# The last group's four tiles go through merge, output, query and routing one by one

## The reference

```python
mix = g[:, :, 0] * (o_sb @ w_br_sb) + g[:, :, 1] * (o_nsa @ w_br_nsa) + g[:, :, 2] * (o_moba @ w_br_moba)
x = layer_norm(DEEPNORM_ALPHA * x + mix @ w_out, ln1_g, ln1_b)
return layer_norm(DEEPNORM_ALPHA * x + peer_ffn(x, peer_wq, peer_k1, peer_k2, peer_u, peer_v), ln2_g, ln2_b)

# peer_ffn, per block of 128 tokens
q = jnp.einsum('td,dhc->thc', xb, w_q)
s1 = jnp.einsum('thc,hkc->thk', q[..., :half], sub_k1).astype(jnp.float32)
s2 = jnp.einsum('thc,hkc->thk', q[..., half:], sub_k2).astype(jnp.float32)
...                                    # top 8 of each, top 8 of their 64 sums: 4 heads x 8 = 32 experts a token
act = jax.nn.gelu(jnp.einsum('thkd,td->thk', u_tab[idx], xb).astype(jnp.float32))
return jnp.einsum('thk,thkd->td', (g * act).astype(v_tab.dtype), v_tab[idx])
```

## Time and profile before

| what | us |
|---|---|
| median of 3 runs | 2807.62 |
| profiled execution, span (first to last instruction) | 2819.9 |
| its own time | the page gives the span alone; the slowest of the three runs is 2830.58 |
| end of the last tile's attention (copy of its output, L1431) | 2456.9 |
| last index stored (L1643) | 2571.8 |
| TensorE, VectorE, ScalarE, GpSimd busy | 2453.4, 1942.6, 786.9, 1233.1 |
| transfers | 777 MB, mean 276 GB/s |

### The profile page before, as it was taken

The page is one execution under the profiler, slowest core; times in us unless marked ns, Lnnn a source line. Parts: engine busy times, 40 slices in busy tenths (PEclk is TensorE's granted clock), DMA queues, the critical chain, the costliest instruction groups (busy, mean ns, idle before and its releaser), DMA issues.

```text
span 2819.9 us, 30185 instructions
## 1 busy us (share of the span) xinstructions
PE 2453.4 (87%) x10632; PEld 1484.2 (53%) x10632; DVE 1942.6 (69%) x4009; ACT 786.9 (28%) x1563; POOL 1233.1 (44%) x1028
## 2 busy tenths in 40 slices
PE   8998998998999989899988887999989999987126
PEld 4764476575445357657654465476445347644012
DVE  0122245588988875667886887587998886687875
ACT  2243222213344332321342212212445333301001
POOL 0000023354565432434553655164656352656775
PEclk9998999999989999999997998999999899999569
DMA  4323258787888776977896999787889685998998
GB/s 144 105 73 100 90 188 337 273 290 253 304 283 302 266 251 224 379 286 270 323 359 246 338 375 350 272 297 255 298 297 330 221 308 200 394 366 317 362 373 320
DMA packets 224183, 776.98 MB, mean 276 GB/s; under 512 B 23200, under 2 KB 39712, under 8 KB 219552
## 3 DMA queue, kind: packets, MB, share of 16 engines
q0 software_dynamic: 147456, 536.94, 52.1%
q1 hardware_dynamic: 73696, 227.80, 22.6%
q10 hardware_dynamic: 2880, 10.31, 0.9%
HBM read 766.56 MB, written 8.39 MB: 275 GB/s over the span
## 4 chain that ended last, share of the span: by engine, by line
PE 57%; DVE 15%; DMA 9%; issue 8%; POOL 7%; ACT 3%; another core or an unknown queue 0%; DVEq 0%; ACTq 0%; SPq 0%
PE ps L1056 14%; PE ps L931 7%; PE ps L900 6%; PE ps L984 6%; PE ps L1089 5%; POOL rows L840 4%; DVE x L1535 4%; DMA rows<-in_table_u,idx 4%; PE ps L886 3%; DMA rows<-in_table_v,idx 3%; PE ps L1124 3%; DVE rows L1520 2%; PE ps L1150 2%; DMA wring<-in_merge 2%; PE ps L993 2%
## 5 line engine op out<-in xcount | busy, mean ns | idle before, releaser
L840 POOL DMA_INDIRECT rows<-in_table_u,idx x462 | 565.2, 1223 | 1021.3 <-DVE idx L1643 506.7
L1056 PE MATMUL ps<-xT,wring 128*128 128x256 f32 x3072 | 768.1, 399 | 56.5 <-DMA wring<-in_merge 24.6
L840 POOL DMA_INDIRECT rows<-in_table_v,idx x434 | 526.5, 1213 | 490.5 <-DVE x L1535 362.4
L1056 PEld LDWEIGHTS ps<-xT,wring 128*128 128x128 f32 x3072 | 586.2, 197 | 245.4 <-issue 90.4
L1520 DVE CUSTOM_DVE_ANT_0 rows<-rows,x 128x1024 f32<-128x1024 f32 x462 | 555.0, 1223 | 120.0 <-DMA rows<-in_table_u,idx 114.3
L1535 DVE SCALAR_TENSOR_TENSOR x<-rows,wts,x 128x1024 f32<-128x1024 f32 x413 | 529.8, 1283 | 65.6 <-DMA rows<-in_table_v,idx 43.6
L1089 PE MATMUL ps<-KA,QA 33*128 33x512 f32 (+7 forms) x576 | 253.7, 537 | 26.5 <-DVE part_m L1777 12.9
L1389 ACT ACTIVATE scratch<-scratch,negm 128x640 f32<-128x640 f32 (+7 forms) x192 | 143.5, 747 | 475.3 <-DVE negm L1777 464.6
L900 PE MATMUL ps<-wring,G 128*128 128x512 f32 x384 | 184.8, 617 | 9.7 <-DVE G L1678 6.3
L1777 DVE CUSTOM_DVE_ANT_0 scratch<-ps,cst 128x128 f32<-128x128 f32 (+3 forms) x192 | 86.9, 454 | 143.0 <-PE ps L1089 140.3
L886 PE MATMUL ps<-oT,wring 128*128 128x256 f32 x384 | 126.0, 464 | 53.0 <-DVE G L1673 35.1
(11 more groups left out here) (209 smaller groups left out, 2951.4 us busy)
## 6 DMA issues: line engine op xcount, KB each, us to landing
wring<-in_merge SPq DMA_DIRECT2D x216, 512.0 KB
wring<-in_w_out_h SPq DMA_DIRECT2D x48, 512.0 KB
wring<-in_w_query SPq DMA_DIRECT2D x32, 512.0 KB
G<-in_w_query SPq DMA_DIRECT2D x12, 1024.0 KB, 8.5
G<-in_x SPq DMA_DIRECT2D x16, 512.0 KB, 4.6
G<-in_ln SPq DMA_DIRECT2D x8, 1024.0 KB, 6.8
G<-x_mid SPq DMA_DIRECT2D x16, 512.0 KB, 5.4
rows<-in_table_u,idx POOLq DMA_INDIRECT x462
```

Of the source, the lines that this page charges most:

```text
L840: pool.indirect_dma_start(row_slot(n), None, tab_u if table == "u" else tab_v, bass.IndirectOffsetOnAxis(ap=idx[:, GT * (g % 2) + t, e:e + ...
L1056: mm = pe.matmul(gate_bank(p)[:, SW * n:SW * (n + 1)], w[:, lo:lo + P], xT[:, kc, SW * (p // HALF_GATES):SW * (p // HALF_GATES + 1)], star ...
```

## The change

The last group has four sections of one tile instead of two of a pair. Tile 12's runs in phase 2, tile 13's in phase 3, tile 14's in phase 4, and tile 15's after the last attention. The gates stay in halves of 256 tokens: the first 12 gate steps go into phases 0 and 1 (six each), steps 12 to 15 into phase 3 behind tile 13's section, 16 to 23 into phase 4 ahead of tile 14's. The tanh stays one for a half. In groups 0 to 2 the whole first section moves into phase 3, the score statistics there take its first half, and the gates 12 to 23 are all in phase 4. Merge follows the tanh at once everywhere. `route` takes its work buffers from a free part of `G` and no longer waits for attention. The last group loads every section's weights through the ring (20 pieces each). The planner's constants change, expert rows of the last group go tile by tile (u, v, u, v), and a tile's gelu follows at the first step of its v block.

```diff
+LAST_GROUP = [(0,), (1,), (2,), (3,)]
+SECTIONS = [(g, tiles) for g in range(NG - 1) for tiles in ((0, 1), (2, 3))] + [(NG - 1, tiles) for tiles in LAST_GROUP]
...
+def home_half(sec):
+    return {"first": 1, "third": 0}.get(role(sec), gate_half(sec))
...
 def early_section():
-    first = [("tanh", 0, 0, 0.0)] + [("gate", 0, (HALF_GATES, part), 0.0) for part in range(PARTS)]
-    first += gate_steps(HALF_GATES + 1) + [("merge", 0, k, 1.5) for k in range(12)] + section_outs(0) + gate_steps(HALF_GATES + 2)
-    second = [("norm", 0, 1, 0.0)] + gate_steps(HALF_GATES + 3)
-    second += [("turn", 0, k, 1.5) for k in range(2 * ST)] + sum([query_steps(0, k) for k in range(4)], [])
-    second += [("match", 0, k, 1.2) for k in range(2 * ST)] + [("route", 0, tt, 0.5) for tt in range(ST)]
-    return first, second + sum([gate_steps(p) for p in range(HALF_GATES + 4, GATES)], [])
+    first = [("tanh", 0, 0, 0.0)] + [("merge", 0, k, 1.5) for k in range(12)] + section_outs(0)
+    first += [("norm", 0, 1, 0.0)] + [("turn", 0, k, 1.5) for k in range(2 * ST)] + sum([query_steps(0, k) for k in range(4)], [])
+    return first + [("match", 0, k, 1.2) for k in range(2 * ST)] + [("route", 0, tt, 0.5) for tt in range(ST)]
...
+def tile_section(s, begin=False):
+    steps = [("tanh", s, 0, 0.0)] if begin else []
+    steps += [("merge", s, k, 1.5) for k in range(6)] + section_outs(s, 1) + [("norm", s, 0, 0.0)]
+    steps += [("turn", s, k, 1.5) for k in range(2)] + sum([query_steps(s, k) for k in range(2)], [])
+    return steps + [("match", s, k, 1.2) for k in range(2)] + [("route", s, 0, 0.5)]
...
-    share = [0, 5, 9, 12]
+    share = [0, 5, 9, 12] if g + 1 < NG else [0, 6, 12, 12]
...
+        elif g + 1 < NG:
+            late = sum([gate_steps(p) for p in range(HALF_GATES, GATES)], [])
+            streams.append((0.0, early_section() if phase == 3 else late, 0.97))
+        elif phase == 2:
+            streams.append((0.0, tile_section(0, True), 0.97))
+        elif phase == 3:
+            streams.append((0.0, tile_section(1) + sum([gate_steps(p) for p in range(HALF_GATES, HALF_GATES + 4)], []), 0.97))
         else:
-            streams.append((0.0, early_section()[phase - 3], 0.95))
+            own = tile_section(2, True) if len(LAST_GROUP) == 4 else []
+            streams.append((0.0, sum([gate_steps(p) for p in range(HALF_GATES + 4, GATES)], []) + own, 0.97))
...
-            streams.append((0.0, row_steps(phase, GT * half + phase), 0.85))
+            streams.append((0.0, row_steps(phase, GT * half + phase), 0.5 if phase == 3 and g + 1 < NG else 0.85))
...
+BLOCKS = [(sec, table, t) for sec, (g, tiles) in enumerate(SECTIONS) for table in ("u", "v") for t in tiles]
...
-            if kind == "tanh" and sec >= NS:
-                nxt = max(nxt, SECTION_STEPS * (sec - NS + 1) + 19)
+            if kind == "tanh" or kind == "merge" and a == 0:
+                nxt = max(nxt, steps_needed(sec))
...
-            now += (.78 if kind in HEAD_KINDS or s < 0 else 1.12 if not late else 1.0 if g % 2 else 1.1) * pe
+            now += (.78 if kind in HEAD_KINDS or s < 0 else 1.12 if not late else 1.05) * pe
             if kind in ("tanh", "turn") and s < 0:
-                ahead = 1.0 if g == NG else TIGHT_AHEAD if kind == "tanh" else EXPERT_AHEAD
+                ahead = TIGHT_AHEAD if kind == "tanh" else EXPERT_AHEAD
+            if g >= NG - 1 and s >= 0 and kind in ("merge", "turn") and role(sec) in ("third", "last"):
+                ahead = 0.5 if kind == "merge" or g == NG else EXPERT_AHEAD
...
-            if kind == "route" and a == ST - 1:
-                ready, started = SECTION_STEPS * (sec + 1), busy + 8.0
-                if s == 0:
+            if kind == "route" and a == len(SECTIONS[sec][1]) - 1:
+                ready, started = 2 * NEXP * tiles_before(sec + 1), busy + 8.0
+                if sec == NS * g and g < NG:
                     times.append(started)
-                    if g == NG - 1:
-                        ahead = 1.0
...
         def piece(sec, kind, k):
-            if SECTIONS[sec][1] > 0:
+            if role(sec) in ("late", "last"):
                 return bank(6 + k % 2)
-            return bank(6 if kind in ("merge", "out") else k % 2)
+            if role(sec) == "third":
+                return bank(k % 2)
+            return bank(6 if role(sec) in ("first", "second") or kind in ("merge", "out") else k % 2)
         def depth(sec, kind):
-            return 1 if SECTIONS[sec][1] == 0 and kind in ("merge", "out") else 2
+            return 1 if role(sec) in ("first", "second") or role(sec) == "early" and kind in ("merge", "out") else 2
...
             def residual(sec):
+                if home_half(sec) != gate_half(sec):
+                    sp.wait_ge(idx_ready, GT * g + tiles[0])
+                else:
+                    sp.wait_ge(x1T_free, sec + 1)
...
+            def ring_section(sec):
+                for b in (2, 1, 0):
+                    load("br", sec, b)
+                if home_half(sec) == gate_half(sec):
+                    residual(sec)
+                for n in range(4):
+                    load("o", sec, n)
+                if home_half(sec) == gate_half(sec):
+                    norm_rows(sec)
+                for n in range(4, 8):
+                    load("o", sec, n)
+                for n in range(8):
+                    load("q", sec, n)
                 load("k", sec)
...
                 for n in GATES_FIRST:
+                    if n == GATES - 4 and role(early[0]) == "first":
+                        residual(early[0])
+                        norm_rows(early[0])
                     load("gate", g, n)
...
                     if n == 2 * GATES - 8:
-                        used(("q", sec, 7))
-                        used(("k", sec))
+                        sp.wait_ge(idx_ready, GT * g + ST)
...
+                        elif role(late[0]) == "third":
+                            residual(late[0])
+                            norm_rows(late[0])
...
-            sp.wait_ge(oT_copied, GT * NG)
-            late_section(NS * NG - 1)
+            for sec in sections_of(NG - 1, 1):
+                ring_section(sec)
...
-                if e == 10 and b > 0:
+                if b > 0 and e == (0 if own_next(b - 1) else 10):
                     expert_finish(b - 1)
...
-            def route(T):
+            def route(sec, T):
-                dve.wait_ge(values_done, pairs_before(GT * g + GT - 1) + 1)
+                home_ = home_half(sec)
+                eqbuf = G[:, 1, home_, 0:512]
+                cand = G[:, 1, home_, 512:768].rearrange("p (h n) -> p h n", h=PH)
```

More of the change, by code:

```diff
@@ L42, with role, sections_of, tiles_before @@
 NS = GT // ST
-SECTIONS = [(g, s) for g in range(NG) for s in range(NS)]
 SW = ST * P
+LAST_GROUP = [(0,), (1,), (2,), (3,)]
+SECTIONS = [(g, tiles) for g in range(NG - 1) for tiles in ((0, 1), (2, 3))] + [(NG - 1, tiles) for tiles in LAST_GROUP]
+LAST = len(SECTIONS) - 1
+def role(sec):
+    g, tiles = SECTIONS[sec]
+    if len(tiles) == 1:
+        return ("first", "second", "third", "last")[tiles[0]]
+    return "early" if tiles[0] == 0 else "late" if g + 1 < NG else "last"
+def sections_of(g, half):
+    return [sec for sec, (own, tiles) in enumerate(SECTIONS) if own == g and tiles[0] // ST == half]
+def tiles_before(sec):
+    return sum(len(tiles) for _, tiles in SECTIONS[:sec])
+def gate_half(sec):
+    return SECTIONS[sec][1][0] // ST
+def home_half(sec):
+    return {"first": 1, "third": 0}.get(role(sec), gate_half(sec))
+def merges_of(sec):
+    return 6 * len(SECTIONS[sec][1])
+def merges_before(sec):
+    return 6 * tiles_before(sec)
+def queries_before(sec):
+    return 2 * tiles_before(sec)
 ITEM = KC * 256
@@ L171, in gate_steps, with section_outs @@
     return [("gate", 0, (p, part), 1.72) for part in range(PARTS)]
-def section_outs(s):
-    out = [[("out", s, (k, part), 1.72) for part in range(PARTS)] for k in range(2 * ST)]
+def section_outs(s, tiles=ST):
+    out = [[("out", s, (k, part), 1.72) for part in range(PARTS)] for k in range(2 * tiles)]
+    if tiles == 1:
+        return out[0] + out[1] + [("mean", s, 0, 0.0)]
     return out[0] + out[1] + out[2] + [("mean", s, 0, 0.0)] + out[3][0:2] + [("norm", s, 0, 0.0)] + out[3][2:4] + [("mean", s, 1, 0.0)]
@@ L215, in head_steps @@
     route = [("route", -1, tt, 0.5) for tt in range(ST)]
-    steps = [("tanh", -1, 0, 0.0)]
     if g == NG:
-        steps += merge + outs + turn[0:2] + norm + turn[2:4]
-        return steps + sum(query, []) + match + route
-    steps += turns[0:2]
+        return pair_section(LAST - NS * NG) if len(SECTIONS[LAST][1]) > 1 else tile_section(LAST - NS * NG)
+    steps = [("tanh", -1, 0, 0.0)] + turns[0:2]
     for n in range(6):
@@ L342, in cost, with steps_needed @@
             "turn": (1.5, 0.0), "query": (1.72, 0.0), "match": (1.2, 0.0), "route": (0.0, 9.0)}[step]
+def steps_needed(sec):
+    g, tiles = SECTIONS[sec]
+    if g == 0:
```

(3 more changed lines are left out.)

332 lines of the change are left out of this document (182 added, 150 removed).

## The result

The changed kernel takes 2921.69 us (median of 4 runs, 2905.25 to 2932.53) against 2806.9 before. The ratio is **1.040**, interval 1.034 to 1.045. Forecast was 2753 us. The profiled execution took 2925.97 us, span 2924.2. The two traces differ by 104 us where the medians differ by 115, since the execution traced before (span 2819.9) lies further above its median.

The account below looks back on a forecast made before the run. TensorE bounds up to 2457 us, DMA after 2572. Attention ends at 2457 + 48 + 24 = 2529, last section 73, 112 rows x 1.417 = 159, + 4: span 2765, 55 below 2819.9; median 2753, range 2713 to 2830.

Parts of the forecast that it names:

- Groups 0 to 2, booked at +19 rows and no time: Groups 0 to 2 route some 45 us earlier, so the plan stands +19 rows (0 to 25) ahead by the last group.
- (b): Last group's stage: merge right behind tanh without gates makes TensorE wait at two places, +6 us (0 to 15).
- Single tiles in the stage: +48: Last group's attention stage: tile 14's section plus splitting tiles 12 and 13, 44 us at the stage's 93%, +48 us.
- New waits in the stage: +24: TensorE in the last group's stage: busier VectorE +8, merge behind tanh +6, later weights +10 us.
- Rows beside attention: Last group's stage: rows filling holes make VectorE busier, costing TensorE +8 us (0 to 12).
- +19 +10 +32 rows: Last group's stage: +19 rows from the filled hole, +10 from the earlier last routing, +32 from attention lasting 72 us longer.
- Weights later: +10 (0 to 40): Attention stage: weights come later as transfers are denser, TensorE waits +10 us (0 to 40) beyond today's 6.5.
- Last section: 73: Tile 15's section after attention, from merge to routing, takes 73 us, with indices at 2602.
- Rest: 112 rows at 1.417: After the last routing 112 expert rows are left at 1.417 us each, 159 us, + 4.
- Rival 2: Transfers bound the attention stage through ring pieces beside gathers; median 2843 (+1.3%), slower by over 1% below 312 GB/s; chance 0.17.
- Rival 3: Short gaps from one-bank pieces lower TensorE's clock from 0.92 to 0.85 over 2067 to 2529; median 2768; chance 0.12.
- The profiled execution: Profile page before the change: its span of 2819.9 was taken for the run of 2830.6, with 10.7 us around it.

Follow-up runs that it names:

- covering run: Changed kernel with other positions in the written order only: attention steps between tanh and merge and between norm and turn, queries' spread ahead of tanh; 2883.82 us, ratio 1.029.
- e_pairs_cover_late: Changed kernel with pairs in the last group, tanh and norm covered by attention steps, last pair's weights loaded as before the change; 2838.98 us, ratio 1.002, slower chip.
- thinned: VectorE works on 128 of 1024 columns of stage rows: old groups 0 to 2 with single-tile last group 2890.16 us (1.017); kernel before 2833.53 us (0.997).
- e_last_small: Old groups 0 to 2, single-tile last group; its stage rows worked on 128 of 1024 columns and gathered at 128 KB instead of 512 KB; 2793.31 us, ratio 0.994.
- lighter run: Old groups 0 to 2, single-tile last group, a quarter of each output and query weight piece of its four sections loaded; 2869.81 us, ratio 1.024.
- repacked pairs: Changed kernel with the last group in two pairs again, laid out like its groups 0 to 2: 2879.87 us, ratio 1.027; with tanh and norm covered: 2839.74 us, 1.009.
- e_lastonly2: Changed kernel's single-tile last group behind groups 0 to 2 laid out as before the change, run as yardstick on another chip; 2885.88 us, ratio 1.028.

## Why the prediction was wrong, step by step

The span was to fall by 55 us and grew by 104, a miss of 159: 57 of it up to the stage, 54 in the stage, 17 in the last section, 31 in the rest. Two steps failed. The repacking of groups 0 to 2 was given no cost, and rows beside attention were given almost none. The other bullets are terms of the sum that were mis-sized, and what was right.

- **Groups 0 to 2, booked at +19 rows and no time**, are the first failed step. I priced only the gain of routing "some 45 us earlier". The first routing came 25 us earlier in group 0, 2 in group 1 and 7 later in group 2. By the plan 21 rows more are indeed done at the end of the last head (599, not 578), but this cost 67 us in this trace, 50 and 54 in the other two of the same groups. The covering run shows 22 to 39 of them as uncovered tanh, norm and the slower clock behind. I had booked (b) at two places of 3 us in the last group; in groups 0 to 2, where the diff takes the same gates away, I booked nothing. And I looked at VectorE's merge, not at ScalarE's queue, where the spread waits behind the tanh. What stays after covering is 28 us by these two traces, and on the slower chip nothing clear (e_pairs_cover_late ends the groups at 1768, the old layout at 1758 to 1771); that inherited rows are its cause is argued, not shown.
- **Single tiles in the stage: +48.** With the rows' work and transfers nearly taken away the stage is 606 us, 47 above the 559 of before with its full rows, so this is a floor for the excess. With 225 rows (before: 230) it is 631, +72. By matmuls the step was nearly right: TensorE is busy 55 us more in that run, where 44 were reckoned. One slip: by columns alone the sum would be 7 us smaller, not 5 (88 matmuls for each of three tiles, 0.027 us each).
- **New waits in the stage: +24.** TensorE is idle 53 us more. The norm's end makes 24 of them, a wait that the sum had only in the last section. The merge product makes 18 (booked: 6) and the spread behind the tanh 7. Covering alone did not shorten the stage, so these waits are where the time shows and not shown to be its cause.
- **Rows beside attention, booked as almost free,** are the second failed step. I counted +19 +10 +32 rows in the stage at 8 us of price, and the other rows as taking idle VectorE time. The last 51 rows (276 against 225) cost the stage 60 us, 1.2 us each; in the tail a row costs 1.4 to 1.5. A row moved forward gains 0.3 to 0.6, not 1.417. The thinned and the small-row runs show that the larger part of the price is in transfers: VectorE's own time is 14 to 33 us, the transfers 52 to 63.
- **Weights later: +10 (0 to 40)** was booked as TensorE waiting for weights. That wait did not grow: 4.4 + 1.1 us in the stage instead of 6.5. The lighter run allows up to 10 us for the weights' bytes by another way, which is within the noise.
- **Last section: 73.** It took 90: 14 us behind tile 14's routing were not in the sum, which had tile 14 routed before the end of attention. Taking about half of that wait away gave nothing, as the wait for weights grew instead. A section of half the work saved 25 us, not 42.
- **Rest: 112 rows at 1.417.** 128 were left (64 + 38 on VectorE, 104/4 = 26 on TensorE) and took 194 us, 1.52 each. Both terms were off, by 23 and 13 us. In its first 40 us the DMA engines are busy at 0.74 only (230 GB/s), and GpSimd waits once 18.5 us there for VectorE to be done with a row; before, the rest began at 0.97 (364 GB/s). TensorE sums 26 of 128 rows instead of 56 of 184, as only one tile is in the last block; that this is why a row costs more is not shown.
- **Rival 2**, transfers as the bound of the stage, named the right place and, at 2843, came nearest. Its sign was the bytes' rate (below 312 GB/s): it was 301 GB/s in the stage, at a DMA share of 0.83, and 307 from 1955 to the end. But its way was weights that land late in the ring, and TensorE waited for those no longer than before; it was VectorE that waited for rows, 56 us instead of 24. Its price was too low, as it had nothing for groups 0 to 2.
- **Rival 3**, the clock: 0.94 became 0.89 in the stage and 0.96 became 0.93 before it. By the rows it follows the waits: where these went (small rows) it was 0.94 again. What the Trainium skill (TensorE: Matmul & The Clock Gate, A second HAM failure mode: psum-queue depth-cycling) says of a bf16 kernel, that short idle spells between groups of matmuls make the clock swing, agrees with these rows; but the spells here were waits for tanh, norm and merge, and tile 14, on two banks, waited 13 us as well.
- **The profiled execution** was taken for the run of 2830.6 us, 10.7 over its span. In every run on record time and span are under 3 us apart, so it was another, of about 2822 us; the forecast did not rest on it.

## What to carry to other kernels

Before work is taken out of a phase, ask which latency it covered, on every in-order queue that the phase's first instructions pass: here gates hid 8 us of tanh on ScalarE and a norm on VectorE. Covering them again took the repacked pairs from 2.7% to 0.9%. Filling an idle engine is not free when its input shares the transfers of the bound engine: price one unit at the margin by moving some out, not by the engine's idle time. Halving a section saves less than half where what sets it is a chain of landings and routings. And follow the routing itself: a section moved ahead in the order, but into busier phases, stored tile 14's index 94 us later than before.

## What the runs showed of the hardware

- A stretch of TensorE with the same 7144 records was busy 1600.6 us at mean clock 0.96 and 1637.1 us at 0.93. With waits of 3 to 9 us in it, it was idle 31 us more and, by its slower matmuls, busy 36.5 us more.
- Cutting VectorE's time per row to a quarter moved an attention stage by 7 to 22 us (16 to 33 with the slower chip allowed for); cutting the row's transfer from 512 to 128 KB as well moved it by 63 (some 52), with the DMA share going from 0.85 to 0.53.
- With the rows' transfers at a quarter, 512 KB weight pieces in the same stage landed in 4.0 to 4.2 us (median) instead of 5.4 to 7.3 (e_last_small and e_lastonly2, on one chip).
